# One inference step on one core: the merge gates' sixteen tiles computed in the prompt's attention, sixteen ring slots for the experts, and three DMAs at other places

## The reference

```python
# 256 prompt rows and 8 sample rows (one new token each), D_MODEL 1024, fp32
p_a, p_b, p_g = split_cols(rms_norm(x) @ w_in, (1792, 1304, 2048))
y_a = rwkv_branch(p_a, ...)                # 8 heads of 64, token shift, per-token recurrence
y_b = nsa_prompt / nsa_sample(p_b, ...)    # compressed, selected and window attention; samples read a
                                           # paged cache and a window state of 511 kept rows each
g_a, g_b = split(sigmoid(p_g), 2)          # the merge gates: 2 x 1024 columns
x = x + (g_a * (y_a @ w_br_a) + g_b * (y_b @ w_br_b)) @ w_out
x = x + moe_ffn(rms_norm(x))               # top 4 of 32 experts: w_up 1024 x 2048, w_down 1024 x 1024
y = rms_norm(x)                            # outputs too: new K/V rows, window state moved by one row,
                                           # recurrent state, last projection row
```

## Time and profile before

| | us |
|---|---|
| median of 3 runs | 1788.57 |
| lowest, highest | 1782.23, 1802.88 |
| the profiled execution | 1795.35 |
| its span, first to last instruction | 1793.5 |

### The profile page before, as it was taken

The page is one execution under the profiler, slowest core; times in us unless marked ns, Lnnn a source line. Parts: engine busy times, 40 slices in busy tenths (PEclk is TensorE's granted clock), DMA queues, the critical chain, the costliest instruction groups (busy, mean ns, idle before and its releaser), DMA issues. The chain is left out here.

```text
span 1793.5 us, 21221 instructions
## 1 busy us (share of the span) xinstructions
PE 1382.3 (77%) x8102; PEld 696.5 (39%) x8103; DVE 372.5 (21%) x792; ACT 224.1 (12%) x479; POOL 169.9 (9%) x226
## 2 busy tenths in 40 slices
PE   6978976499689595497878887887877887877870
PEld 5867876266577484332222222222222222222220
DVE  3341174311333322510101010010101010010104
ACT  2221111022122103210000000000000000000001
POOL 1000061211200000000010100000010100000010
PEclk9989988698556897599999999999999999999995
DMA  5326231531402225299999999999999999999973
GB/s 171 118 87 218 74 76 29 122 107 49 178 1 94 113 100 170 92 370 416 417 418 416 419 415 419 416 418 416 418 416 417 418 415 418 414 418 414 418 282 133
DMA packets 128400, 489.60 MB, mean 273 GB/s; under 512 B 18750, under 2 KB 50752, under 8 KB 94896
## 3 DMA queue, kind: packets, MB, share of 16 engines
q1 hardware_dynamic: 117304, 457.15, 64.8%
q0 software_dynamic: 10640, 31.11, 4.9%
q10 hardware_dynamic: 400, 0.55, 0.1%
HBM read 484.37 MB, written 16.95 MB: 280 GB/s over the span
## 5 line engine op out<-in xcount | busy, mean ns | idle before, releaser
L1964 PE MATMUL bank<-ex_ring,ex_xT 128*64 128x512 f32 x2048 | 495.6, 607 | 138.1 <-DMA ex_ring<-in_w_up 136.5
L1964 PEld LDWEIGHTS bank<-ex_ring,ex_xT 128*64 128x64 f32 x2048 | 126.4, 136 | 478.5 <-DMA ex_ring<-in_w_up 319.3
L1982 PE MATMUL bank<-ex_ring,ex_hT 128*64 128x512 f32 x1024 | 247.1, 604 | 47.3 <-DMA ex_ring<-in_w_down 46.6
L1921 DVE TENSOR_SCALAR ex_g<-bank 128x512 f32<-128x512 f32 x32 | 22.1, 691 | 656.8 <-PE bank L1970 656.8
L460 PE MATMUL bank<-hT,w_group 128*128 128x264 f32 (+1 forms) x656 | 153.9, 397 | 6.0 <-DMA w_group<-in_w_in 5.4
L1982 PEld LDWEIGHTS bank<-ex_ring,ex_hT 128*64 128x64 f32 x1024 | 62.4, 136 | 209.2 <-DMA ex_ring<-in_w_down 128.2
L460 PEld LDWEIGHTS bank<-hT,w_group 128*128 128x128 f32 (+1 forms) x656 | 126.3, 194 | 31.0 <-DMA w_group<-in_w_in 5.8
L1866 POOL DMA_INDIRECT scratch_choice<-ex_y,ex_di x32 | 33.3, 1040 | 675.1 <-ACT ex_y L1896 675.1
L1882 ACT ACTIVATE ex_xT<-bank 128x512 f32<-128x512 f32 x33 | 19.7, 597 | 337.7 <-PE bank L1945 337.7
L1886 ACT ACTIVATE ex_hT<-bank 128x512 f32<-128x512 f32 x32 | 19.1, 597 | 311.2 <-PE bank L1951 301.1
L1896 ACT ACTIVATE ex_y<-bank 128x512 f32<-128x512 f32 x32 | 19.1, 597 | 266.4 <-PE bank L1987 266.4
(11 more groups left out here) (456 smaller groups left out, 1362.0 us busy)
## 6 DMA issues: line engine op xcount, KB each, us to landing
ex_ring<-in_w_up SPq DMA_DIRECT2D x256, 1024.0 KB, 17.2
ex_ring<-in_w_down SPq DMA_DIRECT2D x256, 512.0 KB, 18.2
w_group<-in_w_in SPq DMA_DIRECT2D x20, 1024.0 KB, 5.1
win_rows<-in_state_win_kv SPq DMA_DIRECT2D x8, 512.0 KB, 7.3
w_out_sb<-in_w_out SPq DMA_DIRECT2D x1, 4096.0 KB
choice_rows<-scratch_choice SPq DMA_DIRECT2D x2, 2048.0 KB
out_win_s<-in_state_win_kv POOLq DMA_DIRECT2D x1, 4088.0 KB, 24.2
x<-in_x_prompt SPq DMA_DIRECT2D x4, 512.0 KB
```

The source lines that it names most:

```text
L1921: nc.vector.tensor_scalar(g[:], banks[0][:], 7.0, None, ALU.min).then_inc(S["g_ready"], 1)
L1964: mm = mmul(banks[n // 2][lo:lo + SLOTS, :], B["xT"][:, k % 4, SLOTS * (k // 4):SLOTS * (k // 4) + SLOTS], B["ring"][:, k, 512 * n:512 * n ...
L1982: mm = mmul(banks[4][SLOTS * n:SLOTS * n + SLOTS, :], B["hT"][:, k % 4, SLOTS * (k // 4):SLOTS * (k // 4) + SLOTS], B["ring"][:, 8 + j, D ...
```

## The change

- The merge gates' tiles leave the projection: it ends with tile 24. `hT` is kept. In the prompt's attention SyncE loads the eight groups of gate columns into the first compression weights' buffer (two slots, the third group waits for the first's products). TensorE computes three tiles while the compressed branch's softmax runs, a fourth behind its turns, and then one in each of the units 0 to 11, half of it between scores and turn, half between turn and values. ScalarE evicts them as Tanh of half the value; the merge uses (1 + tanh) and halves once in its copy of the product with `w_out`.
- In the projection the small turns follow the last tiles in another order: last projection row after tile 19, then after tile 24 K/V rows, samples' rows and the four sources, without tiles between. ScalarE takes the square roots after tile 13 instead of after tile 17.
- Page table, constants and row numbers are in the projection.
- The copy of the window state is issued behind the selected rows' gathers in the prompt's attention.
- `ring` has sixteen slots. Even experts' `w_down` lies in 8 to 11, odd ones' in 12 to 15. The route loads `w_down` of expert 0 too, and splits the biases in slots 12 to 15. SyncE's order in the experts is down(1), up(1), then up(e), down(e). The space comes from buffers that share memory: decay blocks and a compression buffer in the gates' part of `pT`, two window buffers in `hT`, the route's rows in the experts' work tiles.

```diff
-                groups = [[12, 13], *(... for j in (4, 6, 0, 2, 8, 10, 18, 20, 22, 14, 16)), [GT], *([j, j + 1] for j in range(MT, NT, 2))]
+                groups = [[12, 13], *(... for j in (4, 6, 0, 2, 8, 10, 18, 20, 22, 14, 16)), [GT]]
...
-                    evicted(10, 18)
+                    evicted(10, 14)
                     for m in range(4):
                         act.wait_ge(kkn, m + 1)
                         nc.scalar.activation(sqk[:, m, :], banks[aux[m]][:, 0:T], ACT.Sqrt).then_inc(kks, 1)
+                    evicted(14, 17)
...
-                    projected(14, 22)
+                    projected(14, 20)
...
+                    projected(20, 25)
                     for i in range(6):
                         t0, n = TILES[i // 2]
-                        if i >= 4:
+                        if i < 4:
+                            pe.wait_ge(sh_ok, i + 1)
+                        else:
                             pe.wait_ge(kv_ok, i - 3)
...
+                    dve.wait_ge(pg_in, 48)
+                    for p in range(8):
+                        ts_(C["idx"][:, p, :], pages[:], 32.0, cols8[:, p:p + 1], ALU.mult, ALU.add).then_inc(C["idx_ok"], 1)
...
+                def _(sp):   # attend_prompt
                     sp.dma_start(cseen[:], a["c_cmp_seen"]).then_inc(cin, 16)
+                    for g in range(NG // 2):
+                        if g >= 2:
+                            sp.wait_ge(mtd, 2 * (g - 1))
+                        c0 = 3096 + 256 * g
+                        sp.dma_start(w[:, g % 2], a["w_in"][0][:, c0:c0 + 256].rearrange("(k p) n -> p k n", p=P)).then_inc(w_in[g % 2], 16)
                     sp.dma_start(sc_["const"][:], a["c_samples"]).then_inc(sc_["in"], 16)
...
+                    pool.dma_start(o["win_s"][0, :, 0:511]..., a["state_win_kv"][0, :, 1:512]...).then_inc(win_copied, 16)
...
+                    def gate(t):
+                        act.wait_ge(mtd, t + 1)
+                        nc.scalar.activation(pT[:, MT + t, :], gate_bank(t)[:, 0:T], ACT.Tanh, scale=0.5).then_inc(mte, 1)
...
+                    def gate(t, lo, hi):
+                        if lo == 0:
+                            pe.wait_ge(w_in[t // 2 % 2], 16 * (t // 4 + 1))
+                            if t >= 2 and t != AHEAD and t != AHEAD + 1:
+                                pe.wait_ge(mte, t - 1)
+                        for kc in range(lo, hi):
+                            mm = mmul(gate_bank(t)[:, 0:T], w[:, t // 2 % 2, kc, P * (t % 2):P * (t % 2) + P], C["hT"][:, kc, :], start=(kc == 0), stop=(kc == KD - 1))
+                        if hi == KD:
+                            mm.then_inc(mtd, 1)
...
+                    for t in range(AHEAD - 1):
+                        gate(t, 0, KD)
                     pe.wait_ge(cp, 1)
...
+                    gate(AHEAD - 1, 0, KD)
                     pe.wait_ge(cpe, 4)
...
                     for i in range(16):
                         if i + 1 < 16:
                             scores(i + 1)
+                        if i < NG - AHEAD:
+                            gate(AHEAD + i, 0, KD // 2)
                         turn(i)
+                        if i < NG - AHEAD:
+                            gate(AHEAD + i, KD // 2, KD)
                         values(i)
...
-                        step(tt_(ta[:, m % 2, :], banks[2 * (m % 2)][:, 0:T], pT[:, MT + m, :], ALU.mult))
+                        step(stt(ta[:, m % 2, :], pT[:, MT + m, :], 1.0, banks[2 * (m % 2)][:, 0:T], ALU.add, ALU.mult))
...
+                    for k in range(8):   # route
+                        sp.dma_start(B["ring"][:, 8 + k // 2, D * (k % 2):D * (k % 2) + D], a["w_down"][0][0, P * k:P * k + P, :]).then_inc(S["ring_in"][8 + k // 2], 16)
...
+                    down(1, 1, False)
                     up(1, True)
-                    down(0, False)
-                    with sp.Fori(2, NEXP) as e:
-                        up(e, True)
-                        down(e - 1, True)
-                    down(NEXP - 1, True)
+                    with sp.Fori(1, NEXP // 2) as pair:
+                        for half in range(2):
+                            up(2 * pair + half, True)
+                            down(2 * pair + half, half, True)
```

143 lines of the change are left out of this document (80 added, 63 removed).

## The result

| | before | after |
|---|---|---|
| median of the runs, us | 1793.72 (4 runs, the profiled one not among them) | 1722.63 (4 runs, the profiled one among them) |
| lowest, highest | 1782.23, 1802.88 | 1718.29, 1728.57 |
| the profiled execution | 1795.35 | 1728.57 |
| its span | 1793.5 | 1726.8 |

The ratio is 0.961, with a 95% interval from 0.954 to 0.968. The forecast of 1716 us lies 7 us under the median, inside its range. Later runs of both kernels on another chip gave 0.965 (0.958 to 0.972).

The account below looks back on a forecast made before the run. Expert weights' DMA bounds the expert stage; ahead of it, TensorE or chains of TensorE, VectorE and ScalarE do. Terms -70 - 3 + 10.5 - 10 = -72.5 give 1723 from the profiled 1795.35 us, 1716 on the median; range 1693 to 1752.

Parts of the forecast that it names:

- Projection, -70: Projection stage: sixteen tiles at 3.56 us and several waits go, less new VectorE wait and cooling; bounds -73 and -64.
- Recurrence, -3: Recurrence stage: page table wait and row numbers gone, three DMAs fewer ahead of the sample state; between 0 and -6.
- VectorE then runs into the stretch in which it and GpSimd block each other: Recurrence: a 0.69 us VectorE product takes 8.76 us, ending with GpSimd's products, whose start comes only 2 us earlier.
- Attention, +10.5: Prompt's attention: +2.5 start, +9 loop tiles, -4 last units if the clock stays, +3 weights; bounds 0 and +31.
- The start: Prompt's attention: with four gate tiles ahead, scores begin between 467 and 473 us, taken as 470 against 467.5: +2.5.
- The weights: Prompt's attention: two gate weight groups meet the window copy and land in 18 us, 13 us ahead of use: +3.
- Experts, -10: Expert stage: weights land earlier at the start, -6.5, and the tail is shorter, -3.2; bounds -14 and -4.
- the tail: Experts, last up slot to last product: 19.9 us in place of 23.0, all weights there: -3.2.
- Half clock throughout: Rival, prompt's attention: TensorE stays at half clock, attention +91.5 in place of +10.5, total 1797 us; chance 0.07.
- Starved weights: Rival, prompt's attention: all six late weight groups land in 18.0 us, +36 in place of +3, total 1749; chance 0.12.
- the projection would not shrink by the tiles: Rival, projection: stores hold the stage's end or TensorE is cold in the small turns: -60, total 1725; chance 0.1.
- the ring would bring nothing: Rival, experts: the weights run dry at the start for as long as was gained, total 1725; chance 0.1.

Follow-up runs that it names:

- before again: The kernel before, unaltered, run a second time on another chip for a second trace: 1792.70 us, ratio 0.999 (0.995 to 1.003).
- the run with three slots: The changed kernel with a third slot for the gates' weights, each group asked for two tiles earlier: 1714.94 us, ratio 0.959 to the kernel before.

## Why the prediction came out, point by point

- **Projection, -70, measured -73.7.** The steps held: no wait for weights, the tile's price, VectorE's copies as the last thing late. The 3 us for cooling were not needed.
- **Recurrence, -3, measured -16.4 (7 to 16 over eleven traces).** Wrong. The step that failed is "VectorE then runs into the stretch in which it and GpSimd block each other", taken as a fixed end that leaves 0 to 6 us. TensorE waited 7.7 us less. And the prediction left out that the stage's waits went with half clock (0.79 over the stage before, in rows that it did not print): that term stood at nothing and was 8.7 us. By what way the early start gets past GpSimd stays open.
- **Compression, 0, measured +18.3.** Wrong by omission: the stage was held to be untouched since no instruction of it changes. Two traces of before and the runs with parts undone show that the loss comes with the change, and the table shows that it is time at half clock. Why is open.
- **Attention, +10.5, measured +16.8 or +27.7, by kind of chip.** The mechanism was right (full clock under gate tiles, half clock in the last four units: 1.97 us where full clock takes 1.00). Mis-sized were three terms. The start was taken as +2.5 and measured +8.5. The time without a late copy was laid out well (467 in before's times is 26.6 us into the stage, and it came at 26.5), but the late copy does not lie beside it, as assumed, it comes on top. The weights were taken as +3 and measured 7 to 16. With no wait at all the loop takes 95.5 us (window copy in the compression), with them 102.8 and 111.4. The tiles themselves were dearer on paper than in the trace: two units take 12.5 us and not 13.3, 5 us over the twelve, which hid a part of the other two. The prediction counted two late groups by a landing of 18.0 us (rows 4); the longest landing here is 26.7 us, and each wait is followed by a half tile that takes 3.89 us in place of 1.95.

```profile
DMA to landing us min/median/max: 4.9/6.7/26.7
```
```profile
400.76 3.89 PE L1250 MATMUL bank<-hT,w_cmp 128*128 128x264 f32 x8 [4.07 <-DMA w_cmp<-in_w_in]
...
421.92 3.89 PE L1250 MATMUL bank<-hT,w_cmp 128*128 128x264 f32 x8 [5.78 <-DMA w_cmp<-in_w_in]
...
436.89 2.05 PE L1250 MATMUL bank<-hT,w_cmp 128*128 128x264 f32 x8
...
449.39 2.05 PE L1250 MATMUL bank<-hT,w_cmp 128*128 128x264 f32 x8
```

- By the Trainium skill (DMA: Bandwidth & Descriptors, section Queues, rings and completion order) taking turns between queues would, by the estimate made of that rule, have left a group 7 to 8 us to land and no wait at all. The trace does not agree: the group asked for while the window copy ran took 26.7 us, and the second wait is for it. The median of 6.7 us is no test of the rule, for most of the groups had no such copy beside them.
- **ScalarE's functions.** Exp (L1166) and Tanh (L1154) alternate in the loop with no load of tables between them (the stage has one, ahead of its first Exp), so the 5.1 us a pair that they might have cost ScalarE did not come. ScalarE in the loop of after:

```profile
440.19 0.49 ACT L1166 ACTIVATE scores<-scores,row_max 128x256 f32<-128x256 f32 x1
...
441.20 0.39 ACT L1154 ACTIVATE pT<-bank 128x264 f32<-128x264 f32 x1 [0.42 <-PE bank L1250]
```

That exp and tanh lie in one set is what the Trainium skill says (ScalarE: Activation LUTs, section Table sets: the hidden batching unit); the trace agrees.

- **Experts, -10, measured -11.9.** Start 4.7 us (6.5 predicted), the tail 4.2 (3.2), and 3.1 us behind the last product, which no term had.
- **The rivals.** Half clock throughout fell: 0.84 over the stage. Starved weights came in part: two waits, not six. That the projection would not shrink by the tiles fell, that the ring would bring nothing too.
- The total held by luck in part: the recurrence's and the compression's misses, -13 and +18, cancel to within 5 us, and the attention's +6 is met by the projection's and the experts' -6. The range was wide enough for each of them, but the first two had no line in it.

## What to carry to other kernels

Where two engines block each other, do not take the end of the stretch as fixed: eight small instructions and three DMAs moved to the stage before brought 7 to 16 us where 3 were expected. One trace is not enough to say why; look whether the next one shows the same instruction caught. Price a wait of TensorE with the half clock behind it: without an 11.8 us wait the stage was 22 to 34 us shorter than in the changed kernel's two traces, and putting one small DMA ahead of four large ones took the wait away. When dense filler work keeps the clock up, spread it thin over the whole loop rather than thick over a part of it, and compare a stage between two traces only after its small delays have been matched.

## What was not expected of the hardware

- After a wait or a run of tiny products, the clock stayed at 1.2 GHz for 3 to 5 us in the two traces of before and for up to 37 us in those of the changed kernel, in the same code with TensorE 100% busy. Two traces of before agreed with each other; variants that differ only in earlier stages did not.
- With six of a gate tile's eight steps in each unit, the clock stood at 2.4 GHz from soon after the one wait for weights to the end of the loop. The same units without gate products ran at 1.2 GHz but for a few: for instance the first one or two of before again, and in the run with three slots two of the four behind the last gate tile.
- VectorE's copy of `cmp_pT` came 7 us late in all traces of two chips and in none of two others, with the same kernel (122.9 and 111.7 us for the stage).
